# Square sums of the latent attention's items as two fp32r parts made by GpSimd, and the norms' first steps in pieces of 512 and 256 tokens

## What is computed

```python
Layer l (same weights for context and latent tokens; context reads only context):
  h += 1/2 * g0 * SwiGLU_a(mod0(RMSNorm h))
  h += g1 * Mixer_l(mod1(RMSNorm h))
  h += 1/2 * g2 * SwiGLU_b(mod2(RMSNorm h))
  even l: bidirectional Mamba-2 SSD head group || multi-head latent attention head group
  odd l:  windowed grouped-query attention (+-WINDOW) with learned per-head sink logit

def rms_norm(t, gain=None):
    y = tf * lax.rsqrt(jnp.mean(tf * tf, axis=-1, keepdims=True) + EPS)
    return y if gain is None else y * gain
def modulate(t, shift, scale):
    return rms_norm(t) * (1 + scale) + shift
# in the even mixer, for the attention group (8 heads, ranks 384 and 256):
    kv = (rms_norm(ckv, kv_norm) @ w_kvb).reshape(bsz, m, MLA_HEADS, MLA_DN + MLA_DV)
    kn, v = jnp.split(kv, [MLA_DN], axis=-1)
    q = (rms_norm(qa, qa_norm) @ w_qb).reshape(bsz, qa.shape[1], MLA_HEADS, MLA_DN + MLA_DR)
    qn, qr = jnp.split(q, [MLA_DN], axis=-1)
    return rms_norm(qn, qn_g), rms_norm(qr, qr_g)     # and kn, kr likewise; qr, kr get rope
```

## Time and profile before

| | |
|---|---|
| median of three runs | 3201.2 us (3196.47, 3201.2, 3203.34) |
| the profiled execution | 3198.16 us, span 3196.4 us |
| mean granted TensorE clock | 0.986 |
| TensorE busy | 3065.2 us, 96% |
| Vector, Scalar, GpSimd busy | 1921.4, 1142.6, 268.7 us |
| chain that ended last | TensorE 53%, Vector 4%, Scalar 1% |

### The profile page before, as it was taken

The page is one execution under the profiler, slowest core; times in us unless marked ns, Lnnn a source line. Parts: engine busy times, 40 slices in busy tenths (PEclk is TensorE's granted clock), DMA queues, the critical chain, the costliest instruction groups (busy, mean ns, idle before and its releaser), DMA issues.

```text
span 3196.4 us, 43546 instructions
## 1 busy us (share of the span) xinstructions
PE 3065.2 (96%) x17705; PEld 2724.1 (85%) x17705; DVE 1921.4 (60%) x2615; ACT 1142.6 (36%) x1760; POOL 268.7 (8%) x321
## 2 busy tenths in 40 slices
PE   5999999999999998899999999999999999999999
PEld 4999999997669895488999989899998887778887
DVE  7754535534442636757777765877787569643333
ACT  5211212367441321235223324533233467642222
POOL 1100000100001005620000001000000100000000
PEclk8999999999999999999999999999999999999999
DMA  6533424232004220012343312233433120023332
GB/s 208 171 112 100 131 61 146 85 94 61 1 1 132 67 60 14 1 34 77 115 125 112 113 52 80 94 101 103 132 106 119 54 66 15 22 85 99 93 98 92
DMA packets 314303, 274.19 MB, mean 86 GB/s; under 512 B 17426, under 2 KB 290057, under 8 KB 313865
## 3 DMA queue, kind: packets, MB, share of 16 engines
q1 hardware_dynamic: 286992, 182.35, 19.1%
q0 software_dynamic: 25488, 89.14, 8.9%
q10 hardware_dynamic: 1641, 0.14, 0.0%
HBM read 263.21 MB, written 8.39 MB: 85 GB/s over the span
## 4 chain that ended last, share of the span: by engine, by line
PE 53%; DVE 4%; ACT 1%; issue 1%; POOL 0%; ACTq 0%; DVEq 0%
PE ps L2277 30%; PE ps L491 16%; PE ps L1507 1%; PE ps L1483 1%; PE ps L1456 1%; DVE hs_lo L2470 1%; PE ps L1202 1%; PE ps L2359 0%; DVE gst L1567 0%; DVE vw_lo L2210 0%; PE ps L1932 0%; DVE ms_s L2501 0%; DVE h_sb L2478 0%; PE ps L1949 0%; PE ps L1108 0%
## 5 line engine op out<-in xcount | busy, mean ns | idle before, releaser
L481 DVE TENSOR_TENSOR w_lo<-ring,w_hi 128x1024 fp32r<-128x1024 f32 (+3 forms) x221 | 252.2, 1142 | 463.5 <-ACT w_hi L466 374.7
L491 PE MATMUL ps<-u_hi,w_hi 128*128 128x384 f32 (+2 forms) x1584 | 466.6, 354 | 19.4 <-DVE u_lo L652 17.8
L491 PE MATMUL ps<-u_hi,w_lo 128*128 128x384 f32 (+2 forms) x1584 | 462.0, 351 | 0.0
L491 PE MATMUL ps<-u_lo,w_hi 128*128 128x384 f32 (+2 forms) x1584 | 461.8, 351 | 0.0
L466 ACT CAST w_hi<-ring 128x1024 fp32r<-128x1024 f32 (+3 forms) x157 | 149.5, 953 | 555.8 <-PE ps L491 553.5
L491 PEld LDWEIGHTS ps<-u_hi,w_hi 128*128 128x128 f32 x1584 | 285.1, 189 | 45.5 <-issue 22.1
L491 PEld LDWEIGHTS ps<-u_lo,w_hi 128*128 128x128 f32 x1584 | 285.6, 189 | 22.2 <-issue 1.4
L2204 ACT CAST vw_hi<-ring 128x1024 fp32r<-128x1024 f32 (+1 forms) x176 | 181.2, 1031 | 342.0 <-PE ps L2277 280.8
L491 PEld LDWEIGHTS ps<-u_hi,w_lo 128*128 128x128 f32 x1584 | 285.2, 189 | 21.0
L2210 DVE TENSOR_TENSOR vw_lo<-ring,vw_hi 128x1024 fp32r<-128x1024 f32 (+1 forms) x176 | 211.0, 1200 | 152.1 <-ACT vw_hi L2204 151.8
L2277 PE MATMUL ps<-u_hi,vw_hi 128*128 128x384 f32 x768 | 248.4, 337 | 12.8 <-DVE u_lo L652 12.3
(11 more groups left out here) (353 smaller groups left out, 5830.6 us busy)
## 6 DMA issues: line engine op xcount, KB each, us to landing
ring<-in_w_ff_in SPq DMA_DIRECT2D x176, 512.0 KB, 3.9
ring<-in_w_ff_out SPq DMA_DIRECT2D x72, 512.0 KB, 4.0
cst<-in_w_mod POOLq DMA_DIRECT2D x72, 512.0 KB, 3.9
m_in<-in_w_mod POOLq DMA_DIRECT2D x56, 512.0 KB, 4.0
ring<-in_w_in_e SPq DMA_DIRECT2D x26, 512.0 KB, 3.9
m_first<-in_w_mod POOLq DMA_DIRECT2D x16, 512.0 KB, 15.2
ring<-in_w_out_e SPq DMA_DIRECT2D x16, 512.0 KB, 3.8
ring<-in_w_ff_out SPq DMA_DIRECT2D x16, 384.0 KB, 3.5
```

The costliest lines, as they stand in the source:

```text
L481: dve.tensor_tensor(w_lo[:, b:b + WIDE[n]], ring[:, s:s + WIDE[n]], w_hi[:, b:b + WIDE[n]], ALU.subtract).then_inc(w_split_lo, 1)
L491: mm = pe.matmul(ps_at(p, c0, c1) if halved else pair(p)[:, c0:c1], w, x[:, c0:c1], start=start and i == 0, stop=stop and i == 2)
```

## The change

1. **Norms in pieces.** For n = 1 to 4 the channel sum, Ln, Exp and the first block's multiplication go in two pieces, tokens 0 to 512 and 512 to 768, each with its own semaphore step, so that Scalar's Ln of the first piece starts before TensorE has summed the second. Blocks 1 to 7 are multiplied whole as before. n = 0 and n = 5 have one piece.
2. **High part first.** At every seam TensorE begins with the products that need only `u_hi` of a block (with `w_hi` and `w_lo`) and puts the one with `u_lo` behind them (`pe_first_two`, and the same in `pe_s_plain_chunk`).
3. **Squares in parts.** For items 6 to 25 GpSimd casts `sqh` to fp32r and subtracts; TensorE sums both parts in fp32r (four matmuls in place of two fp32 ones), behind the products of item m+2 instead of m+1. Ln, Exp, norm and rope follow one step later too.
4. **Raw copies of qn and kn on Vector** instead of Scalar (`qr` stays on Scalar). The rope's three semaphores become one.

```diff
+        def hi_products(pe, p, n, k, hi, t, start):
+            b = (n % 2) * SLOT + P * k
+            for w in (w_hi, w_lo):
+                for c0, c1 in cuts(t) if t == T else ((0, t),):
+                    pe.matmul(ps_at(p, c0, c1) if t == T else pair(p)[:, c0:c1], w[:, b:b + P], hi[:, c0:c1],
+                              start=start and w is w_hi, stop=False)
+        def pe_first_two(pe, n, run, p0, p1, t, free):
+            for k in range(DB + 1):
+                if k == 0:
+                    free(0)
+                    pe.wait_ge(w_split_lo, n + 1)
+                if k < DB:
+                    pe.wait_ge(n_u, 8 * run + k + 1)
+                    hi_products(pe, p0, n, k, u_hi[:, k], t, k == 0)
+                if k == 1:
+                    free(1)
+                    pe.wait_ge(w_split_lo, n + 2)
+                if k:
+                    mm = three_products(pe, p1, n + 1, k - 1, u_hi[:, k - 1], u_lo[:, k - 1], t, k == 1, k == DB)
+                if k < DB:
+                    pe.wait_ge(n_lo, 8 * run + k + 1)
+                    mm = lo_products(pe, p0, n, k, u_lo[:, k], t, k == DB - 1)
+                if k >= DB - 1:
+                    mm.then_inc(w_used, 1)
...
-            act.wait_ge(n_ss, n)
-            act.activation(RSN[n][:, :t], pair(3, t), ACT.Ln, bias=eps, scale=1.0 / D).then_inc(n_ln, 1)
-            act.wait_ge(n_ln, n + 1)
-            act.activation(RSN[n][:, :t], RSN[n][:, :t], ACT.Exp, scale=-0.5).then_inc(n_rs, 1)
+            for i, (t0, t1) in enumerate(NORM_SEGS[n]):
+                act.wait_ge(n_ss, SS_TO[n - 1] + i + 1)
+                act.activation(RSN[n][:, t0:t1], pair(3)[:, t0:t1], ACT.Ln, bias=eps, scale=1.0 / D).then_inc(n_ln, 1)
+                act.wait_ge(n_ln, RS_TO[n - 1] + i + 1)
+                act.activation(RSN[n][:, t0:t1], RSN[n][:, t0:t1], ACT.Exp, scale=-0.5).then_inc(n_rs, 1)
...
-                m = q - 1
-                if m == m1 - 1:
+                if q == m1:
+                    for m in summed(q, m0, m1)[:-1]:
+                        pe_item_sum(pe, m, m0, norm_n)
                     (pe_v_e if m0 == 0 else pe_v_o)(pe, 0, 0, 2)
-                if m0 <= m < m1:
+                    pe_item_sum(pe, m1 - 1, m0, norm_n)
+                else:
+                    for m in summed(q, m0, m1):
+                        pe_item_sum(pe, m, m0, norm_n)
+
+        def pe_item_sum(pe, m, m0, norm_n):
                     it = items[m]
-                    pe.wait_ge(hn_sq, m + 1)
+                    if parts_of(m):
+                        pe.wait_ge(hn_sqlo, m - FIRST_PARTS + 1)
+                    else:
+                        pe.wait_ge(hn_sq, m + 1)
...
+                        if parts_of(m):
+                            w = sum_w[:, P:2 * P] if WIDTH[it["kind"]] == 64 else sum_w[:, 0:P]
+                            pe.matmul(pair(2)[:, c0:c1], w, sqh_hi[m % 2][:, c0:c1], start=True, stop=False)
+                            mm = pe.matmul(pair(2)[:, c0:c1], w, sqh_lo[:, m % 2, c0:c1], start=False, stop=True)
+                        else:
...
+        FIRST_PARTS = 6
+        def parts_of(m):
+            return FIRST_PARTS <= m < n_even
+        def summed(q, m0, m1):
+            x = [m for m in (q - 2, q - 1) if m0 <= m < m1 and q == m + 1 + parts_of(m)]
+            if q == m1 and parts_of(m1 - 1):
+                x.append(m1 - 1)
+            return x
+        def pool_item_parts(pool):
+            pool.wait_ge(hn_sq, FIRST_PARTS + 1)
+            pool.tensor_copy(sum_w[:, 0:P], ones).then_inc(hn_sqhi, 1)
+            pool.tensor_copy(sum_w[:, P:2 * P], blk64).then_inc(hn_sqhi, 1)
+            pool.wait_ge(u_kept, 32 * DB)
+            for m in range(FIRST_PARTS, n_even):
+                pool.wait_ge(hn_sq, m + 1)
+                pool.tensor_copy(sqh_hi[m % 2][:, 0:T], sqh[:, m % 2, :]).then_inc(hn_sqhi, 1)
+                pool.wait_ge(hn_sqhi, m - FIRST_PARTS + 3)
+                pool.tensor_tensor(sqh_lo[:, m % 2, :], sqh[:, m % 2, :], sqh_hi[m % 2][:, 0:T],
+                                   ALU.subtract).then_inc(hn_sqlo, 1)
...
-                    act.activation(dst, src, ACT.Identity, scale=gain_of(it)).then_inc(hn_raw, 1)
+                    if it["kind"] not in RAW_BY_DVE:
+                        if q and items[q - 1]["kind"] in RAW_BY_DVE:
+                            act.wait_ge(hn_raw, q)
...
+            for q in range(m0, m1 + 1):
+                if q < m1:
+                    if items[q]["kind"] in RAW_BY_DVE:
+                        dve_raw(dve, q)
+                    if q < m1 - 1:
+                        dve_split(dve, base + q - m0 + 3)
...
+                for m in summed(q, m0, m1) if q >= FIRST_PARTS else [m for m in (q,) if m < FIRST_PARTS]:
+                    if m < FIRST_PARTS and q >= FIRST_PARTS:
+                        continue
+                    if items[m]["stop"]:
+                        dve_head_norm(dve, m)
+                    if m and items[m - 1]["rope"]:
+                        dve_rope(dve, items[m - 1])
```

More of the change, by code:

```diff
@@ L9 @@
+import itertools
 from contextlib import ExitStack
@@ L493, in three_products, with lo_products @@
             return mm
+        def hi_products(pe, p, n, k, hi, t, start):
[4 more added lines that the diff above has]
+                              start=start and w is w_hi, stop=False)
+        def lo_products(pe, p, n, k, lo, t, stop):
+            b = (n % 2) * SLOT + P * k
+            for c0, c1 in cuts(t) if t == T else ((0, t),):
+                mm = pe.matmul(ps_at(p, c0, c1) if t == T else pair(p)[:, c0:c1], w_hi[:, b:b + P], lo[:, c0:c1],
+                               start=False, stop=stop)
+            return mm
+        def pe_first_two(pe, n, run, p0, p1, t, free):
[16 more added lines that the diff above has]
+                    mm.then_inc(w_used, 1)
         def read_as(p, x, t):
@@ L609, in pe_norm @@
             for c0, c1 in cs:
[L610 to L611 removed]
+                pe.matmul(pair(3)[:, c0:c1], ones, SQN[n][:, 1, c0:c1], start=False, stop=True).then_inc(n_ss, 1)
             if n in MODS_AT:
@@ L645, in dve_scale @@
                 dve.wait_ge(n_lo, 8 * run + d - 3)
-            dve.tensor_tensor(normed(n, d)[:, :t], h[:, d, :t], RSN[n][:, :t] if n else pair(3, t), ALU.mult).then_inc(n_t, 1)
+            for i, (t0, t1) in enumerate(NORM_SEGS[n] if d == 0 else ((0, t),)):
+                if d == 0:
+                    dve.wait_ge(n_rs, RS_TO[n] - len(NORM_SEGS[n]) + i + 1)
+                dve.tensor_tensor(normed(n, d)[:, t0:t1], h[:, d, t0:t1], RSN[n][:, t0:t1] if n else pair(3, t),
+                                  ALU.mult).then_inc(n_t, 1)
         def dve_low(dve, n, run, d):
@@ L1149, in dve_items, with dve_raw @@
             dve_split(dve, base + 2)
-            for m in range(m0, m1):
-                if m < m1 - 1:
-                    dve_split(dve, base + m - m0 + 3)
-                if items[m]["stop"]:
-                    dve_head_norm(dve, m)
-                if m0 < m < m1 - 1 and items[m - 1]["rope"]:
-                    dve_rope(dve, items[m - 1])
+            for q in range(m0, m1 + 1):
[4 more added lines that the diff above has]
+                        dve_split(dve, base + q - m0 + 3)
+                if m0:
+                    if q < m1 and items[q]["stop"]:
+                        dve_head_norm(dve, q)
+                    if m0 < q < m1 - 1 and items[q - 1]["rope"]:
+                        dve_rope(dve, items[q - 1])
+                    continue
+                for m in summed(q, m0, m1) if q >= FIRST_PARTS else [m for m in (q,) if m < FIRST_PARTS]:
+                    if m < FIRST_PARTS and q >= FIRST_PARTS:
+                        continue
+                    if items[m]["stop"]:
+                        dve_head_norm(dve, m)
+                    if m and items[m - 1]["rope"]:
+                        dve_rope(dve, items[m - 1])
+        def dve_raw(dve, q):
+            it = items[q]
+            t = it["t"]
+            dve.wait_ge(hn_sq, q + 1)
+            if it["kind"] == "kn" and it["i"] == 0:
+                dve.wait_ge(u_kept, 32 * DB)
+            if q and items[q - 1]["kind"] not in RAW_BY_DVE:
+                dve.wait_ge(hn_raw, q)
+            dst, src = read_as(q % 2, dst_of(it)[:, :t], t)
+            dve.tensor_scalar(dst, src, gain_of(it), None, ALU.mult).then_inc(hn_raw, 1)
         def dve_head_norm(dve, m):
@@ L2287, in pe_s_plain_chunk @@
                 if o < 2:
-                    pe.wait_ge(n_lo, run + kk + 1)
-                for e in range(2):
-                    mm = pe_s_products(pe, [(bank(first[e], 0, ht), 0, ht), (bank(second[e], 0, ht), ht, t)], c, 256 * k + P * e,
-                                       u_hi[:, kk], u_lo[:, kk], kk == 0, kk == 7)
-                    if k == 3:
-                        mm.then_inc(q_done, 1)
+                    pe.wait_ge(n_u, run + kk + 1)
+                for low in range(2):
+                    if o < 2 and low:
```

(10 more changed lines are left out.)

76 lines of the change are left out of this document (29 added, 47 removed).

## The result

The changed kernel takes 3212.1 us in the median of six runs (3208.59 to 3214.41), the kernel before 3201.59 (3196.47 to 3203.34). The ratio is 1.0029, with a 95% interval of 1.0019 to 1.0040: **9.3 us slower**, 6 to 13. Its profiled execution took 3208.59, span 3206.8.

The account below looks back on a forecast made before the run. It took TensorE, busy 96% of the span, as the bound; seams −7.1 and items +16.6 gave +9.5 on the profiled 3198.2, so 3207.7, or 3210.7 against the median, said as 3211 us; range 3195 to 3223.

Parts of the forecast that it names:

- two large terms: The seams before the norms' products, forecast at −7.1 us, and the items, forecast at +16.6 us.
- the rope steps: Four kn items beside qr ropes, Vector's raw copy behind each rope: 28.3 us against 14.9, so +13.4.
- the low clock: TensorE's clock falling in idle gaps: nothing in the sum, 2 us in the range's upper end.
- a sum saves 0.6: Each of 20 item sums on TensorE takes 0.69 us instead of 1.30, −12 if TensorE stays the bound.
- My limit of 4.0: A qn loop's own limit from GpSimd's and Vector's instructions taken in turn: 4.0 us, above TensorE's 3.8 but near it.
- Seam starts: TensorE's first products behind the norm sum at n=1 to 4 start 2.3 us earlier: pieces 1.2, high part first 1.1.
- What n=1 and n=4 keep: At these seams item 0 completes 1.04 us later in the new order, so 1.25 of 2.3 is gained at each.
- n=0 and n=5 give nothing: At these one-piece seams TensorE's start hangs on w_lo, for which nothing changes: gain zero.
- Seams together: Gains of 2 × 2.3 and 2 × 1.25 at n=1 to 4: −7.1 us, bounds −4.8 and −8.
- Items together: Start and qn loops about +1, kn items beside ropes +13.4, last four kn +2.2: +16.6 us.
- the second rope step: Every other kn item beside a qr rope: Vector's 4.83 us plus three GpSimd instructions of 4.5, so 9.33.
- The rule of exclusion: Vector instructions with two SBUF operands and GpSimd instructions run one after the other: ledger at least +9.3 us in the items.

Follow-up runs that it names:

- the seams alone: Kernel before plus only norms in pieces and high part first (fp32 sums, raw copies on Scalar): ratio 0.9989 to the kernel before, 3.5 us faster.
- seams_early: Kernel before plus norms in pieces and high part first, but the last block's low product ahead of the second column's: ratio 0.9982 to the kernel before.
- short_rope: Changed kernel with the four qr ropes cut to 16 of 512 tokens: ratio 1.0015 to the kernel before, items 93.2 us.
- psum_operand: Changed kernel with one operand of Vector's norms (items 6 to 20) and qr rope arithmetic read from PSUM: ratio 1.0022 to the kernel before, items 94.9 us.
- raw_only: Changed kernel with fp32 sums instead of GpSimd's parts, raw copies of qn and kn still on Vector: ratio 1.0008 to the kernel before, items 90.9 us.

## Why the prediction was right, point by point

The sum was +9.5 against the profiled execution, measured +10.4 there and +9.3 by the ratio. Its two large terms hold in kind and sign. That the total came so near is luck in part: within them the rope steps were put too dear by 3.5, and the low clock, which the sum had at nothing, cost some 5.0 by its rows (below). The profiled execution has luck of its own: from the norm n=3 to the norm n=4 it took 545.1 where the execution before took 550.4, and the seam explains 2.0 of these 5.3.

- **TensorE is the bound and a sum saves 0.6.** Right where no rope is near: 3.83 a loop, and no idle time. My limit of 4.0 for GpSimd and Vector together did not bite, but it was near: between 728 and 745 GpSimd's subtractions start every 3.90, and its wait for the next Square shrinks from 0.75 to 0.47. The loops ended before it was used up.
- **Seam starts.** 2.3 forecast, 2.02 measured at each of n=1 to 4; pieces 1.02 (1.2 said) and high part first 0.89 when alone (1.1 said).
- **What n=1 and n=4 keep.** 1.25 each forecast: 2.3 less 1.04 for the order. Measured is 2.02 less the wait of 0.88, so 1.14. Counted to item 0's sum, n=1 kept 1.3 and n=4 0.5 in the changed kernel, and nothing at n=4 in the run of the seams alone; that spread comes from the granted clock of single executions, as the rows in the experiments show. The mechanism, item 0's Square behind a cast that waits for `w_used`, is what `seams_early` removed.
- **n=0 and n=5 give nothing.** The reason given was wrong. The last row is the third column of weights, not TensorE's start; the start stands 14.4 earlier and is ended by `u_lo`:

```profile
2824.28 0.77 PE L491 MATMUL ps<-u_hi,w_hi 128*128 128x512 f32 x1 [4.48 <-DVE u_lo L652]
```

  With the change the start at n=5 is 0.63 earlier, but the wait at the third column is 1.86 instead of 1.19, and from the norm's sum to the end both kernels take the same (377.7 and 377.9). At n=0 more is lost: from TensorE's first product to the sum of n=1 the changed kernel took 569.1, the seven other kernels with its order of products 568.2 to 569.4, the kernel before 566.8 and the two others with the old order 567.0 and 567.3. I had said that nothing changes for `w_lo`. It does: the first column is complete three pairs later, as at n=1, and the wait for the third column is 1.41 instead of 0.38. So 1.0 of the 2.3 is the order (0.2 was gained in front of it). The other 1.5 is TensorE's busy time behind that wait (547.7 instead of 546.2 for the same matmuls), with two stretches at the lower clock instead of one; whether the order causes the second is not shown. With the order mended the stretch is 567.0.
- **Seams together**: −7.1 forecast; −5.9 in the trace without n=0 and n=5, −3.5 (0.6 to 6.4) by the ratio of the seams alone. It was over-sized by the 0.3 at each start and by the 2.3 at n=0.
- **Items together**: +16.6 forecast, +16.2 in the trace. Up to the product of item 18 it is +2.7 (said +1); the four steps with ropes take 24.8 (said 28.3, before 14.9); from there to the last sum 18.5 (said 17.0, before 14.8).
- **The mis-sized term is the second rope step.** I put 9.33 for it, 4.83 and all of three GpSimd instructions. The raw copies stand at 759.68, 765.19, 772.19 and 777.70: 5.5 and 7.0. The rows above show why: only the subtraction falls wholly into the rope (2.31 − 0.68 = 1.6), the cast half (0.5), and the third instruction runs beside the raw copy, which excludes nothing. But the other step, which I had at 4.83, was 0.7 longer, because its split of weights waited for the end of that third instruction (1.10 at 760.61, 0.41 at 766.12). A couple of rope steps so took 12.5 instead of 14.2. TensorE's idle time at the first four kn was 9.4, forecast 13.
- **The clock.** The sum had nothing for it; I allowed 2 in the range's upper end only. It was 0.90 over the stage, and in three stretches its cost can be read off, because TensorE did not wait behind the slow products until its next sum: 1.7 at 704.22 and 1.7 at 720.97 (4.82 and 4.81 for nine pairs, full 3.12), and 1.6 at 790.32 (5.14 to the next sum; `short_rope` does the same matmuls in 3.51 at the full clock). What TensorE waited for behind the first two depended in turn on its own products: Vector's split at 713.69, ahead of the norm and the rope of kr, had waited 1.88 for Scalar's cast, and that 0.71 for TensorE. Together that is 5.0 of the 16.2, and it accounts for the two places where the items were dearer than said: the first two lie before the product of item 18, where +2.7 would be −0.7 without them, and the last behind the ropes, where 18.5 would be 16.8. The cost to the stage is still read off rows and not shown by a run with another clock. Beside the ropes the low clock cost 1.9 at 760.74 and 1.7 at 773.25 (4.00 and 3.75 for six pairs, full 2.08), but there the next thing TensorE waited for was Vector, whose row ran without a pause, so these may have cost nothing.
- **The rule of exclusion**, weighed against one row before, is shown by `psum_operand`, and its condition with it. But I made too much of it: taken away from norms and ropes it gives back 4.5 of 16.2. The longer row of Vector (raw copy, four-step rope beside the shorter kn), GpSimd's 2.66 an item, and the low clock behind the waits that these make do the rest.

What stays open is how much of the items' 16 belongs to the moved raw copy in the changed kernel's exact order (3.4 if GpSimd's work stays; `raw_only`'s 7.7 has another order), how much of it a full clock would give back, and what makes the granted clock, and with it the unchanged stages, vary by some 3 us either way from execution to execution.
